# Moving a group norm's sums of squares into the next turn of a state-space stage

## The reference, cut to what matters

```
u = rmsnorm(x, norm_w) @ w_in                 # split into z, x/B/C, dt
xbc = silu(conv4(xbc))                        # x, B, C of each of 8 groups
y   = ssd_scan(x * dt, a, B, C) + x * d_skip  # in chunks of 128 positions
y   = y * silu(z)
yg  = y per group of 256 channels
yg  = yg * rsqrt(mean(yg * yg) + eps)         # the group norm
out = x + (yg * gnorm) @ w_out
```

## Time and profile before

| what | value |
|---|---|
| time, median of 3 runs | 1743.27 us (1741.03 to 1745.18) |
| the profiled execution's own time | 1753.72 us |
| span of the profiled execution, first to last instruction | 1752.1 us |
| TensorE busy in the span | 1530.1 us (87%) |
| VectorE, ScalarE, GpSimd busy | 714.5, 527.7, 108.1 us |
| mean granted clock of TensorE, as a share of full speed | 0.913 |

### The profile page before, as it was taken

One profiled execution on the slowest core, in us unless ns is written; L12 is line 12 of the kernel. 1 busy time (PEld: TensorE's weight loads), 2 busy tenths in 40 slices (PEclk: granted clock), 3 DMA queues, 4 the chain that ended last, 5 costly groups with the idle time before them and its releaser, 6 DMA issues. The chain is left out here.

```text
span 1752.1 us, 22951 instructions
## 1 busy us (share of the span) xinstructions
PE 1530.1 (87%) x8057; PEld 1191.9 (68%) x8057; DVE 714.5 (41%) x1824; ACT 527.7 (30%) x945; POOL 108.1 (6%) x147
## 2 busy tenths in 40 slices
PE   6989999999998898998997998997684888888587
PEld 3867788777876687786766775874452656666375
DVE  2046755765576102000452263154363444444412
ACT  4134235423432111002333233134342333433102
POOL 0021111112111000000001001001000000000000
PEclk7989999999997897998998998998687898989888
DMA  6074454525442270116006106202302555553111
GB/s 182 3 210 154 109 152 156 170 74 171 147 128 92 75 192 1 31 42 157 25 1 157 48 1 144 61 0 57 89 1 66 153 135 137 151 158 99 51 57 49
DMA packets 141544, 170.20 MB, mean 97 GB/s; under 512 B 46532, under 2 KB 108348, under 8 KB 141132
## 3 DMA queue, kind: packets, MB, share of 16 engines
q1 hardware_dynamic: 130120, 129.38, 26.2%
q0 software_dynamic: 11344, 39.79, 8.3%
HBM read 149.20 MB, written 24.32 MB: 99 GB/s over the span
## 5 line engine op out<-in xcount | busy, mean ns | idle before, releaser
L274 PE MATMUL psum<-arena 128*128 128x260 f32 x1536 | 357.6, 390 | 7.5 <-DMA arena<-in_ssd_w_in 7.5
L1481 PE MATMUL psum<-arena 128*128 128x260 f32 x1408 | 332.9, 394 | 7.8 <-DMA arena<-in_nsa_w_in 5.4
L274 PEld LDWEIGHTS psum<-arena 128*128 128x128 f32 x1536 | 292.5, 193 | 61.3 <-DMA arena<-in_ssd_w_in 7.9
L1481 PEld LDWEIGHTS psum<-arena 128*128 128x128 f32 x1408 | 268.1, 194 | 64.5 <-issue 13.0
L327 PE MATMUL psum<-arena 128*128 128x128 f32 (+9 forms) x1371 | 202.8, 293 | 96.1 <-DVE arena L1768 24.0
L327 PEld LDWEIGHTS psum<-arena 128*128 128x128 f32 (+9 forms) x1371 | 157.9, 150 | 149.4 <-issue 57.6
L1051 PE MATMUL psum<-arena 128*128 128x260 f32 x656 | 149.8, 392 | 6.7 <-PEq L595 4.8
L1051 PEld LDWEIGHTS psum<-arena 128*128 128x128 f32 x656 | 128.1, 196 | 27.9 <-issue 7.2
L1186 PE MATMUL psum<-arena 128*128 128x252 f32 x512 | 123.9, 404 | 5.3 <-ACT arena L1181 5.3
L1186 PEld LDWEIGHTS psum<-arena 128*128 128x128 f32 x512 | 103.7, 205 | 22.5 <-issue 4.8
L1693 ACT ACTIVATE arena<-arena 128x128 f32<-128x128 f32 (+3 forms) x128 | 71.9, 562 | 134.5 <-DVE arena L1785 129.5
(11 more groups left out here) (261 smaller groups left out, 1633.5 us busy)
## 6 DMA issues: line engine op xcount, KB each, us to landing
arena<-in_cache_kv SPq DMA_DIRECT2D x128, 256.0 KB, 4.4
arena<-in_ssd_w_in SPq DMA_DIRECT2D x16, 1024.0 KB, 5.5
arena<-in_nsa_w_in SPq DMA_DIRECT2D x16, 1024.0 KB, 5.4
arena<-scr_rows POOLq DMA_DIRECT2D x16, 520.0 KB, 6.6
arena<-in_ssd_w_in SPq DMA_DIRECT2D x16, 512.0 KB
arena<-scr_rows POOLq DMA_DIRECT2D x8, 1024.0 KB, 6.6
arena<-in_state_ssm POOLq DMA_DIRECT2D x16, 512.0 KB, 7.2
out_ssm_sample<-arena POOLq DMA_DIRECT2D x16, 512.0 KB, 7.2
```

Source lines behind the costliest of these rows:

```text
L274: mm = nc.tensor.matmul(psum[:, b + h, 0:HALF], w[:, k, n % 2 * P:(n % 2 + 1) * P], xn[:, k, h * HALF:(h + 1) * HALF], start=(k == 0), sto ...
L1481: mm = nc.tensor.matmul(psum[:, pair + h, 0:HALF], w[:, k, at * P:(at + 1) * P], xn[:, k, h * HALF:(h + 1) * HALF], start=(k == 0), stop=( ...
```

## The change

The four products that sum the squares become a function `group_sums(g)`. It is no longer called at the end of a turn, but in the next turn, between the first and the second half of that turn's first tile. The logarithm and the exponential become `group_std(g)`, called in the next turn behind the three SiLUs and the exponential of the decays, ahead of the first copy of a projection tile out of PSUM. Behind the last turn both are called once for the last group. On ScalarE turns 1 and 2 are now written out and the loop has two passes (turns 3 to 6), since the first call has one wait fewer.

```
 # TensorE, turn(i, j, more, first)
                 nxt(0, 0)
+                if not first:
+                    group_sums(i - 1)
                 nxt(0, 1)
                 nxt(1, 0)
...
                 nxt(5, 1)
-                pe.wait_ge(sqg_done.sem, sqg_done.at(i, 1))
+            def group_sums(g):
+                pe.wait_ge(sqg_done.sem, sqg_done.at(g, 1))
                 for h in range(2):
                     for q in range(2):
                         mm = nc.tensor.matmul(psum[:, 6 + h, 0:HALF], ones, ytmp[:, q, h * HALF:(h + 1) * HALF],
...
             turn(SG - 1, 1, more=False)
+            group_sums(SG - 1)

 # ScalarE, turn(i, j, more, first, second)
                 nc.scalar.activation(eexp, pairs[:, :, 1, :], ACT.Exp).then_inc(e_ready.sem, 1)
+                if not first:
+                    group_std(i - 1, second)
                 nxt(0)
...
                 nc.scalar.activation(ytmp, y, ACT.Square).then_inc(sqg_done.sem, 1)
-                act.wait_ge(ssg_full.sem, ssg_full.at(i, 1))
+            def group_std(g, first=False):
+                act.wait_ge(ssg_full.sem, ssg_full.at(g, 1))
                 if not first:
-                    act.wait_ge(yt_done.sem, yt_done.at(i, 0))
+                    act.wait_ge(yt_done.sem, yt_done.at(g, 0))
                 nc.scalar.activation(gstd.rearrange("p (h t) -> p h t", h=2), halves(psum, 6), ACT.Ln, bias=epsc,
                                      scale=1.0 / 256).then_inc(varg_done.sem, 1)
-                act.wait_ge(varg_done.sem, varg_done.at(i, 1))
+                act.wait_ge(varg_done.sem, varg_done.at(g, 1))
                 nc.scalar.activation(gstd, gstd, ACT.Exp, scale=-0.5).then_inc(stdg_done.sem, 1)
...
             turn(0, 0, first=True)
-            with act.Fori(0, SG // 2 - 1) as i:
+            turn(1, 1, second=True)
+            turn(2, 0)
+            with act.Fori(1, SG // 2 - 1) as i:
                 turn(i * 2 + 1, 1)
                 turn(i * 2 + 2, 0)
             turn(SG - 1, 1, more=False)
+            group_std(SG - 1)
```

More of the change, by code:

```diff
@@ L796, in last_tap, with turn @@
                 ins.then_inc(done.sem, 1)
-            def turn(i, j, more=True, first=False):
+            def turn(i, j, more=True, first=False, second=False):
                 def nxt(n):
```

## The result

The changed kernel took 1737.0 us (median of 7 runs, 1726.2 to 1742.0), the kernel before, run beside it, 1745.2 (7 runs, 1741.0 to 1755.6). The ratio is 0.9939, with a 95% interval from 0.9912 to 0.9966: some 6 to 15 us, 10.6 in the middle.

What follows compares the result with a forecast made beforehand. TensorE, busy for 87% of the span, was taken as the bound. Five turns gaining 1.80 (9.0), turn 5 nothing, turn 7 losing 0.9 and 0.6 net 7.5 us: 1743.3 − 7.5 = 1735.8, own range 1733.5 to 1738.5, wider range 1731 to 1742.

Steps and rivals of the forecast that it cites:

- The sums no longer wait; an ordinary turn gains 1.80: TensorE at turn boundaries: half a tile covers ScalarE's square, the idle 1.65 goes, transposes start 1.80 us earlier.
- The logarithm is covered by 0.6: ScalarE's moved logarithm, which the transposes wait for, is seen by TensorE 0.6 us before it reaches them; cost nothing.
- the rival that rested on a slower chain: ScalarE's chain to the logarithm becomes the bound, table loads costing 1.28 more each: 13 us lost, 1756; chance 0.05.
- Normalising is late, at no cost: VectorE's normalising waits for the exponential, making VectorE about 0.1 us late, hidden under TensorE's next two half tiles.
- Turn 5 gains nothing: Ahead of turn 5 VectorE's delayed multiply of x sets the transposes' start: gain 0, bounds 0 and 1.80.
- Turn 3 keeps its 1.80: Ahead of turn 3 VectorE's multiply, after a 4.72 us delay, is just early enough, so the 1.80 us is kept.
- The partial rival: Later logarithm or longer VectorE delay at turn 3 cuts a boundary's gain by 0.4 to 1.8; 1738.5 to 1741.5; chance 0.17.
- Turn 7 loses 0.9 and 0.6: Turn 7: transposes wait for the logarithm, delaying VectorE's additions, 0.9 us; a lower clock after longer idle, 0.6 us.
- E: The moment TensorE's last half tile of a turn ends; times at each turn boundary are counted from it.
- The second term: Turn 7: TensorE's clock likely falls right after the longer idle ahead of the transposes; 0.6 us, between 0 and 2.
- The wait did move: Rival: TensorE comes earlier but waits as long at the transposes as it did at the sums; 1742 to 1745; chance 0.08.
- The larger gain: Rival: turn 7's additions slip out of GpSimd's way, removing the idle 3.43 and low clock; 1726 to 1731; chance 0.08.

Runs made afterwards that it cites:

- sums placed later: Changed kernel with the sums three half tiles into the turn, right ahead of the transposes, instead of one; ratio to the kernel before 0.9997.
- copy earlier: Changed kernel with SyncE's 1 MB copy of a sample's window issued ahead of the wait for tile 6; ratio to the kernel before 0.9931.
- GpSimd late: Changed kernel; in turn 7 GpSimd's multiply of the samples' states waits until VectorE's chunk states are done; ratio to the kernel before 0.9928.

## Why the prediction was right, point by point

*The sums no longer wait; an ordinary turn gains 1.80.* Right, and 0.12 too small: 1.92 at each of turns 1, 2 and 4, and turn 6 has the same 8.77 between sums and transposes. The idle 1.65 and the overlap at both sides of the sums add to it: from the start of the sums to the next record it is 1.75 (336.68 − 334.93) where I kept the 1.86 of before.

*The logarithm is covered by 0.6.* Right. It ended 0.74 before the transposes, where the working, without the quarter microsecond for the signal, had 0.84. The run with the sums placed later shows what this cover is worth. The table loads cost their row, and the rival that rested on a slower chain did not appear. Nor did the drain of some 1380 ns that goes with each switch of tables by the Trainium skill ("ScalarE: Activation LUTs", section "What ACT_TABLE_LOAD costs"): the load at 333.19 starts 0.01 after the square has ended, and its activation 1.30 after the load's start.

*Normalising is late, at no cost.* Right: VectorE waited 40.3 us in the stage for the exponential, and the stretch between transposes and the next wait of TensorE did not grow.

*Turn 5 gains nothing.* Right: 60.73 before and after.

*Turn 3 keeps its 1.80.* Wrong; this is the step that failed. The sum took VectorE's delay at the loop's return as 4.72 us because one profile had it so. It was 7.04 after, and turn 3 took 60.79, 0.43 more than the 60.36 it had. In the second profile of before the delay was 6.98 and the turn took 60.70, so with equal delays turn 3 gains nothing, like turn 5. The partial rival had named it, at nearly its price (up to 1.8 at a boundary, measured 2.2). With the loop written out the delay vanishes, so it belongs to the return; that it stands behind transfers is supported and not settled.

*Turn 7 loses 0.9 and 0.6.* The first was mis-sized a little: the transposes wait 2.59 for the logarithm and start at 520.63. The last half tile ends at 509.19, so that is E + 11.44 against E + 10.80, a loss of 0.64. As forecast, one more pair of operations stands behind GpSimd's multiply: VectorE's second multiply by the decay is held up instead of the third. The second term, a lower clock right behind that idle time, did not come in the two profiles of the changed kernel. It did come in three others with the same idle 2.58 (sums placed later, copy earlier, GpSimd late), and there the chunk states started 7.3 to 7.4 after the transposes instead of 5.8: 1.5 to 1.6, where I took 0.6 within bounds of 0 and 2. Against the spread of 4 us in the rest of turn 7 neither can be read from the runs.

*The sum.* By rows: 4 × 1.92 − 0.43 − 0.64 = 6.6 us, where the working had 7.5. That the two are so close is partly luck: the ordinary turns gave 0.5 more than their terms, turn 3 2.2 less, turn 7 0.9 more. The profiled executions differ by 14.1 in span; the other 7.5 lie in turn 7 behind its transposes (4.1), behind the stage (2.3) and ahead of turn 1 (1.1), stretches that differ as much between executions of the same code. The runs give 10.6 and 10.1 in two measurements, with intervals that reach down to 5.9 and 6.5. That 6.6 is the whole effect is compatible with them, and that a few more come from elsewhere is not excluded.

*The rivals.* The wait did move at two boundaries of seven, turns 3 and 7, and stayed at turn 5. The slower one would have needed a chain 2.4 us longer than summed; it was within 0.1 of it. The larger gain did not come of itself: it took the further edit that puts GpSimd out of the way.

## What to carry to other kernels

An engine that waits for another at the end of a loop's turn loses nothing if a piece of the next turn's work can stand between; count from both sides, since the piece must be long enough ahead of the moved step, and something must be left behind it to cover the chain that hangs on its result. Before costing the new position at nothing, look for delays that end shortly before the engine arrives today: a cover of 2 us hides them, and shortening the arrival uncovers them. For an effect below 1%, compare stretches with equal ends in the traces, over two profiles of each kernel; spans of single executions mix in more than the effect.

## What the runs showed of the hardware that was not expected

VectorE stood still for 4.49 to 7.05 us at each of the 18 returns of its hardware loop in nine profiles, with one transfer of the instruction queue in each gap; the values lie near 4.6 and near 7.0, and none between. ScalarE's and TensorE's loops return at the same places in the kernel before, without such a gap. Written out, VectorE had none, and in the changed kernel each turn took 0.47 us less besides.

After idle times of 2.0 us and more TensorE's granted clock often fell to 0.50, but not each time: behind the idle 2.59 of turn 7 it stayed at 1.00 in the changed kernel and fell in the run with GpSimd late (idle 2.58), with the same instructions ahead of it. Their windows, first the changed kernel, whose transposes start at 520.63, then the other, where they start at 517.93:

```profile
521.00:523.00 2.00, 2.00 (x20) 2.00 (x19) 0.44 (x1) 1.51 (x2) 0.00 (x0) 1.00 1.51 537
523.00:524.00 1.00, 1.00 (x7) 0.85 (x6) 1.00 (x3) 0.60 (x1) 0.00 (x0) 1.00 1.30 508
```

```profile
520.00:522.00 2.00, 2.00 (x9) 1.83 (x9) 1.89 (x4) 0.59 (x1) 0.00 (x0) 0.50 0.49 186
```
